# Trimming the third column chunk of the projections from 364 to 360 columns, with 64-row last tiles

## What is computed

```python
def _even_layer(x, past, norm_g, w_in, w_lr, b_lr, sinks, gla_g, w_out):
    h = _rmsnorm(x, norm_g)
    z = h @ w_in
    aq, ak, av, bq, bk, bv, blr, gate = _split(z, SPLIT_EVEN)
    ...
    ao = _sink_alibi_attention(qb, kb, vb, key_ok, sinks).reshape(b, tl, A_WIDTH)
    glog = jax.nn.log_sigmoid((blr @ w_lr + b_lr).astype(jnp.float32)) / B_GATE_NORM
    bo, s_new = _gla(...)
    bo = _rmsnorm(bo, gla_g).reshape(b, tl, B_WIDTH).astype(x.dtype)
    y = jnp.concatenate([ao.astype(x.dtype), bo], axis=-1) * jax.nn.silu(gate)
    return x + y @ w_out, new_k, new_v, s_new

def _odd_layer(x, hist, h0, norm_g, w_in, conv_w, conv_b, w_ra, b_ra, w_ri, b_ri, lam, w_out):
    h = _rmsnorm(x, norm_g)
    xb, gate = _split(h @ w_in, (C_WIDTH, C_WIDTH))
    ...                      # causal convolution of width 4 gives u
    rg = jax.nn.sigmoid(_blockdiag(u, w_ra, b_ra).astype(jnp.float32))
    ig = jax.nn.sigmoid(_blockdiag(u, w_ri, b_ri).astype(jnp.float32))
    ...                      # gated recurrence by a scan gives hs
    y = hs.astype(x.dtype) * jax.nn.silu(gate)
    return x + y @ w_out, new_conv, hs[:, -1]
```

## Time and profile before

| | us |
|---|---|
| median of 3 runs | 1613.17 |
| lowest, highest | 1612.19, 1615.75 |
| profiled execution, its own time | 1621.99 |
| its span from first to last instruction | 1620.2 |

### The profile page before, as it was taken

How to read it: one execution, slowest core, us unless ns; L and a number is a source line. 1 busy time by engine, 2 the same in 40 slices (tenths; PEclk the granted TensorE clock), 3 DMA queues, 4 the chain that set the end, 5 groups by cost and what they waited for, 6 DMA issues and landing times.

```text
span 1620.2 us, 23515 instructions
## 1 busy us (share of the span) xinstructions
PE 1503.4 (93%) x9332; PEld 1427.1 (88%) x9332; DVE 853.2 (53%) x1181; ACT 450.4 (28%) x766; POOL 685.3 (42%) x461
## 2 busy tenths in 40 slices
PE   6999999999879979899999999889999999989994
PEld 6998878787679969789988999889999999989994
DVE  7113555557564555537255101487887878793114
ACT  5112434435522221221151000315335151560000
POOL 5253222221123324314235444436566665656651
PEclk9999999999889989999999999999999999999996
DMA  4311010100000101011101332111111111122222
GB/s 178 103 59 40 27 42 27 42 27 27 19 29 33 31 32 39 31 32 41 34 26 56 106 107 94 67 39 40 53 53 53 42 49 53 53 69 93 80 79 111
DMA packets 27416, 89.77 MB, mean 55 GB/s; under 512 B 3600, under 2 KB 6736, under 8 KB 27344
## 3 DMA queue, kind: packets, MB, share of 16 engines
q1 hardware_dynamic: 16560, 60.34, 11.1%
q10 hardware_dynamic: 10784, 28.39, 5.3%
HBM read 77.16 MB, written 11.68 MB: 55 GB/s over the span
## 4 chain that ended last, share of the span: by engine, by line
PE 72%; DVE 11%; issue 8%; POOL 5%; ACT 3%; DMA 1%; POOLq 0%; DVEq 0%; ACTq 0%; SPq 0%
PE ps L342 43%; PE ps L507 11%; PE ps L389 6%; POOL w_hi L313 3%; POOL w_lo L317 2%; PE ps L477 2%; PE ps L443 2%; DVE arena L1194 2%; PE ps L464 2%; DVE Y L1445 1%; PE ps L575 1%; PE ps L580 1%; PE ps L564 1%; DVE arena L1463 1%; DVE arena L1507 1%
## 5 line engine op out<-in xcount | busy, mean ns | idle before, releaser
L313 POOL TENSOR_TENSOR w_hi<-raw,ones 128x512 fp32r<-128x512 f32 x228 | 338.7, 1486 | 881.5 <-PE ps L342 539.9
L342 PE MATMUL ps<-H,w_hi 128*128 128x364 f32 x2832 | 580.0, 332 | 34.4 <-DVE H L1035 19.5
L342 PEld LDWEIGHTS ps<-H,w_hi 128*128 128x128 f32 x2832 | 486.7, 189 | 41.4 <-issue 22.6
L342 PE MATMUL ps<-H,w_lo 128*128 128x364 f32 x1752 | 389.2, 331 | 0.0
L317 POOL TENSOR_TENSOR w_lo<-raw,w_hi 128x512 fp32r<-128x512 f32 x228 | 347.9, 1526 | 17.9
L342 PEld LDWEIGHTS ps<-H,w_lo 128*128 128x128 f32 x1752 | 307.9, 190 | 0.0
L342 PE MATMUL ps<-Yr,w_hi 128*128 128x364 f32 x672 | 150.0, 332 | 0.0
L507 PE MATMUL ps<-H,w_hi 128*128 128x364 f32 x672 | 146.7, 338 | 0.0
L389 PE MATMUL ps<-w_hi,H 128*128 128x256 f32 (+1 forms) x720 | 130.7, 282 | 7.3 <-POOL w_lo L317 6.6
L1367 DVE TENSOR_TENSOR arena<-ps,arena 128x1092 f32 (+1 forms) x16 | 20.7, 1295 | 219.2 <-PE ps L342 219.2
L507 PEld LDWEIGHTS ps<-H,w_hi 128*128 128x128 f32 x672 | 112.4, 189 | 12.0 <-issue 10.4
(11 more groups left out here) (174 smaller groups left out, 1720.5 us busy)
## 6 DMA issues: line engine op xcount, KB each, us to landing
raw<-weights SPq DMA_DIRECT2D x114, 512.0 KB, 3.4
arena<-xT ACTq DMA_DIRECT2D x15, 546.0 KB, 4.7
x_scratch<-arena ACTq DMA_DIRECT2D x8, 546.0 KB, 5.3
arena<-x_scratch ACTq DMA_DIRECT2D x8, 546.0 KB, 3.6
yT<-arena ACTq DMA_DIRECT2D x8, 546.0 KB, 2.9
arena<-k_scratch ACTq DMA_DIRECT2D x8, 304.0 KB, 4.8
k_scratch<-Y ACTq DMA_DIRECT2D x2, 512.0 KB, 2.7
arena<-xT SPq DMA_DIRECT2D x1, 546.0 KB, 5.0
```

What stands on the lines that cost most here:

```text
L313: pool.tensor_tensor(w_hi[:, s, cols].rearrange("p (k n) -> p k n", n=P), raw[:, s, cols].rearrange("p (k n) -> p k n", n=P), every_tile_ones,
L342: mm = pe.matmul(sets[st][:, c, 0:CW], lw[:, s, w], rx[:, k, c * CW:(c + 1) * CW], start=(first and n == 0 and m == 0), stop=(last and n = ...
```

## The change

The third chunk of a projection takes 360 columns, the live ones, in place of 364: `cw(c)` gives the width, in `project` and in `fill`. The projections of U (`wide=True`) keep 364, since the convolution shifts the sample tokens into the last columns. The four columns that are no longer written, 360 to 363 of banks 2 and 5, are set to zero once, by a VectorE memset at the start, for which TensorE waits. The last token tile has 64 rows in place of 68 in `sum_squares`, `project_v`, and in the two engines' small steps on the row sums (`norm_roots`, `norm_factors`). All else, the number of matmuls and what the other engines read, stays.

```diff
+        def cw(c):
+            return LIVE - 2 * CW if c == NCH - 1 else CW
...
+        pad_zeroed = sem("pad_zeroed")
...
-            def project(s, kts, piece, rhs_hi, rhs_lo, st, first=True, last=True, at0=0, ready=None, half_end=3):
+            def project(s, kts, piece, rhs_hi, rhs_lo, st, first=True, last=True, at0=0, ready=None, half_end=3,
+                        wide=False):
...
                         for c in range(NCH):
-                            mm = pe.matmul(sets[st][:, c, 0:CW], lw[:, s, w], rx[:, k, c * CW:(c + 1) * CW],
+                            n_cols = CW if wide else cw(c)
+                            mm = pe.matmul(sets[st][:, c, 0:n_cols], lw[:, s, w], rx[:, k, c * CW:c * CW + n_cols],
...
                 for t in range(NT):                                  # sum_squares
-                    m = TOK - SEQ if t == NT - 1 else P
+                    m = tile_rows(t)
...
                 for t in range(NT):                                  # project_v
-                    m = TOK - SEQ if t == NT - 1 else P
+                    m = tile_rows(t)
...
             pe.wait_ge(ones_set, 1)
+            pe.wait_ge(pad_zeroed, 1)
...
                     for c in range(NCH):                             # fill
-                        mm = pe.matmul(sets[0][:, c, 0:CW], lw[:, 1 - n % 2, k * P:(k + 1) * P],
-                                       rx[:, k, c * CW:(c + 1) * CW], start=(x == 0), stop=(x == 3 * KD - 1))
+                        mm = pe.matmul(sets[0][:, c, 0:cw(c)], lw[:, 1 - n % 2, k * P:(k + 1) * P],
+                                       rx[:, k, c * CW:c * CW + cw(c)], start=(x == 0), stop=(x == 3 * KD - 1))
...
                         project((p + 2 * m) % 2, kts, piece + 3 + 2 * m, U_hi, U_lo, v % 2, at0=4 * n,
-                                half_end=None).then_inc(piece_done if n else half_done, 1)
+                                half_end=None, wide=True).then_inc(piece_done if n else half_done, 1)
...
-                act.activation(rT[0:TOK - SEQ, NT - 1:NT], rT[0:TOK - SEQ, NT - 1:NT], ACT.Sqrt).then_inc(std_done, 1)
+                act.activation(rT[0:DEC, NT - 1:NT], rT[0:DEC, NT - 1:NT], ACT.Sqrt).then_inc(std_done, 1)
...
             dve.memset(rT[:, :], 1.0).then_inc(rt_init, 1)
+            dve.memset(ps[:, 2:6:3, cw(NCH - 1):CW], 0.0).then_inc(pad_zeroed, 1)
...
-                parts = [(slice(0, P), slice(0, NT - 1)), (slice(0, TOK - SEQ), slice(NT - 1, NT))]
+                parts = [(slice(0, P), slice(0, NT - 1)), (slice(0, DEC), slice(NT - 1, NT))]
```

## The result

The changed kernel took 1618.88 us (median of nine runs, 1618.01 to 1620.92). The kernel before, run beside it, took 1615.01 us (nine runs, 1611.24 to 1615.75). The ratio is 1.0028, with a 95% interval of 1.0019 to 1.0037: slower by some 4.5 us (the two medians lie 3.9 us apart). I had forecast 1610.8 us, and the range, 1608.3 to 1615.4, does not hold it.

The account below looks back on a forecast made before the run. TensorE's moving columns were taken to set the pace. Narrowing -3.1 us, row sums +0.75, padding and values nothing: -2.35 us, so 1613.17 us became 1610.8, range 1608.3 to 1615.4.

Parts of the forecast that it names:

- The zeroed padding: VectorE's added memset at the start and TensorE's wait for it: covered by 7 us of other waiting, costed at nothing.
- -2.35: Net of all terms for the whole kernel, in us: 3.1 gained by narrowing, 0.75 lost in the row sums.
- Narrowing: Third chunks of projections: 1.84 ns saved on each of 2088 matmuls, 3.1 us of 3.84 taken to reach the end.
- as I had written for L1471: Odd layer: TensorE's pieces finish early and wait for VectorE's and ScalarE's elementwise work, 8.2 us in all.
- Row sums: Three calls with 64-wide f32 weights: entering and leaving that form costs about 0.25 us, 0.75 us lost in all.
- Values: Five value-projection calls with 64-row last tiles in fp32r: nothing gained or lost; bound 0.12 us a call on entry.
- A: Projections: the pace does not follow four columns, only the switches' cost remains, 1613.9 us; chance 0.13.
- B: Whole kernel: all 3.84 us of narrowing arrive and the switches are free, 1609.3 us; chance 0.22.
- C: Value projections: 64-wide fp32r tiles take two passes, 2.4 us a tile; 1615.6 us with two calls exposed; chance 0.07.
- a shift of waits that I did not see: Anywhere in the kernel: remainder left for an unseen shift of waits, in either direction; chance 0.05.
- 603 starts: Wait-free 100 us of TensorE: about 603 matmul starts in place of 601, 0.37%, if the narrowing works.

Follow-up runs that it names:

- e2_dve: Kernel before plus one VectorE memset of unused elements at the start, with no wait on it: 1618.98 us, 1.0025.
- e1_memset: Kernel before plus only the memset of the four columns in two banks and TensorE's wait for it: 1618.23 us, 1.0025.
- e2_act: The whole change, with the padding zeroed by ScalarE in place of VectorE: 1615.84 us, 1.0007 against the kernel before.
- e2_realign: The whole change, with two old VectorE memsets merged so that VectorE issues as many instructions as before: 1615.81 us, 1.0002 against the kernel before.
- the control: The kernel before, unchanged, profiled a second time and used as the trace to compare with: 1614.58 us, 0.9996; span 1614.0 us.
- e3_best: Kernel before plus the narrowing, with 68-row last tiles and the padding zeroed by two VectorE memsets, one a bank: 1614.07 us, 0.9996.
- e1_rows64: Kernel before with only the 64-row last tiles; all chunks keep 364 columns and nothing is zeroed: 1614.98 us, 1.0007.
- e3_w352: The change with ScalarE zeroing and the third chunk cut to 352 columns: 1612.94 us, 0.9988 against the kernel before.
- e4_w362: The change with ScalarE zeroing and a third chunk of 362 columns, run once: 1616.93 us, beside 1616.28 for the kernel before.
- e4_w340: The change with ScalarE zeroing and a third chunk of 340 columns, run once: 1600.07 us, beside 1616.28 for the kernel before.

## Why the prediction was wrong

**The zeroed padding: the step that failed.** "I cost it at nothing", I wrote, with "the cover is 7 us; without it the price would be 0.07 us". The cover is there and the memset does take 0.07 us. But I priced the instruction by its time and its wait, and not by what it does to the instructions behind it. It moves every later VectorE instruction one place on in the stream, and there the saves that release TensorE start late: 2.7 to 3.0 us in the gated heads in all four kernels that have just this shift, nothing like it in the others. By the ratios the shift costs 4.0 us (e2_dve and e1_memset, 1.0025 each). The traces of single executions show 2.1 and 2.5 us at their last matmul; between these and the ratios lies the scatter of single traces in the other stretches, and I cannot assign the rest. Against the sum it is the whole sign: -2.35 became +3.9 between the medians, about +4.5 by the ratio. But it is not the whole miss: without the shift (e2_act, 1.0007) the forecast gain is not there either.

**Narrowing: right in its mechanism, mis-sized twice.** The term was 1.84 ns a third chunk and 3.1 us on the path. The runs show 1.1 to 1.5 ns at this width where nothing waits. In the out-projection and the last projection, 814 third chunks, that is 0.9 to 1.0 us measured (the changed kernel, e2_act, e2_realign) where the term gives 1.5. In the odd layer nothing can be seen (0.07 to 0.31 us more than the control in the four kernels whose clock falls there as often as the control's), and I had taken 78% of all third chunks as on the path; at 320 columns 17.25 of 38 to 40 us arrive, 43 to 45%. At 360 columns e3_best has the narrowing without the loss: its ratio is a gain of 0.6 us, between 2.9 gained and 1.6 lost by its interval, in place of the 3.1. I had read the chain as if its share stayed the same when TensorE gets faster. The other waits took it over, as I had written for L1471, but with more than I gave it. At four columns that wait shows nothing yet. In the changed kernel it is

```profile
PE ps L348 <- DVE Y L1479: 8.2, 7, 2.3
```

as in the earlier trace rows.

**Row sums: a little too dear in themselves, but the clock behind them was left out.** Start to next projection in the control, first call:

```profile
45.93 1.96 PE L362 MATMUL ps<-ones,arena 128*128 128x1 f32 x18
47.76 0.75 PE L342 MATMUL ps<-H,w_hi 128*128 128x364 f32 x3
```

and in e1_rows64:

```profile
46.87 2.04 PE L362 MATMUL ps<-ones,arena 128*128 128x1 f32 x18
48.85 0.77 PE L342 MATMUL ps<-H,w_hi 128*128 128x364 f32 x3
```

1.83 against 1.98 us: 0.15 for entering and leaving the 64-wide form, and the same in the second call; I had 0.25. The call at the end takes 0.26 us more. The sum is 0.56 us in place of 0.75. What the sum lacks stands behind the first call: in e2_act the granted clock falls there, in the control it does not. From 49.0 to 52.5 us (length, PE busy with matmuls touched, granted clock, DMA share, GB/s) in e2_act:

```profile
49.00:52.50 3.50, 3.50 (x14) 0.52 0.00 1
```

and in the control:

```profile
49.00:52.50 3.50, 3.50 (x23) 1.00 0.03 7
```

By the starts of matmuls 186 and 217 it costs 1.1 to 1.5 us. Four of the ten traces with 64-row tiles have it (e2_act, e2_realign, e3_w352, e4_w362) and none of the eight with 68-row tiles. That the 64-row form brings it is likely, then, but no run was made to show it, and the changed kernel's own trace is without it.

**Values: nothing, as forecast.** Where a value projection of the changed kernel reaches its last tile, 68 rows before and 64 now:

```profile
458.95 0.40 PE L395 MATMUL ps<-w_hi,H 128*128 128x256 f32 x2
459.18 0.28 PE L395 MATMUL ps<-w_lo,H 128*64 128x256 f32 x1
...
459.65 0.40 PE L395 MATMUL ps<-w_hi,H 128*64 128x256 f32 x2
```

Six steps take 0.70 us across the change of width, 0.117 each. The Trainium skill (PSUM — Partial Sum Buffer, The four PSUM rules) remarks that float32r matmuls force all column groups. The steps fit that, though no run shows the column groups themselves.

**The rivals.** A (the pace does not follow four columns) was too strong, yet nearest in its effect: e2_act and e2_realign, the change without the shift, stand at 1.0007 and 1.0002. B fell with the odd layer. C, the only one that ended slower by more than 0.75 us, fell with the pace of the 64-row values. What did happen was in none of them; it sat in the 0.05 for "a shift of waits that I did not see". In the stretch of 100 us I had expected 603 starts; the counts there cannot tell it: the control touches 602 matmuls and e2_act 604. Matmuls 5280 to 6180 can: their 149.9 us got 0.33 us shorter, 0.22% where the prediction had 0.37%. The two ends of its range do not follow from its terms: B less half the scatter of the runs (1.8 us) is 1607.5 and not 1608.3, and C with two calls exposed was 1615.6 and not 1615.4. Neither moves the result into the range.

**What stays open.** That the late save stands at a seam of VectorE's instruction supply is read from 18 traces; that the crossing is what takes the 0.35 us fits all of them, but no run moves the seam by itself, and why it takes that long is not shown. Nor is it shown why some widths lie off the line (362 brings nothing in the last projection and 0.7 ns a third chunk between matmuls 5280 and 6180).

## What to carry to other kernels

Cost an added instruction not only by its duration and its cover: it moves everything behind it on its engine, and an instruction that releases the bottleneck may land where it starts a few tenths of a microsecond late; the test is cheap, one idle instruction more or less on that engine. When a part of a change that should be free carries all of the loss, run that part alone, and then an empty stand-in for it. And hold single traces against a second trace of the same kernel before subtracting them: here one chance event of 6 us in the trace of before had the sign of the difference turned round.

## What was unexpected of the hardware

One more VectorE instruction at the start made a save 490 us later start 0.50 us after the matmul that it waits for, in place of 0.15; two more made it 0.15 again. The Trainium skill (Runtime: NRT & Kernel Launch, Instruction fetch mechanics) says that engines are fed with instructions in blocks by a DMA queue of their own, at a cost that is mostly hidden. The packet of the `instruction` queue that follows VectorE's 703rd record in every trace fits this. No run here shows that the supply is the cause; if it is, it is not hidden where the 704th record releases TensorE.

A wait of TensorE that was 0.35 us longer (1.03 in place of 0.68) was followed by a stretch at the lower clock level that cost 1.5 us in 144 matmuls, in all four kernels with the late save (25.71 to 25.76 us by the chain) and in none of the others with 360 or 364 columns (24.19 to 24.23). But e4_w340 has the same fall there after a wait of 0.68 us, without a late save. Its projections behind the first and the second head:

```profile
486.21 25.23 PE ps L348 x144
597.18 23.70 PE ps L348 x144
```

So the longer wait is not needed for the fall, and that it set it off in the four kernels is likely, not shown. With it a wait of 0.35 us came to cost 1.8.
